# Routing ranks and counts in three wide products in place of nine narrow ones

## What is computed

```python
g_idx = jnp.argmax(g_logits, axis=-1)
e_sel = e_logits[rows, g_idx]
top_v, top_i = lax.top_k(e_sel, TOP_K_INNER)          # 2 of the 4 experts of the group
top_w = jax.nn.softmax(top_v, axis=-1) * g_w
e_idx = g_idx[:, None] * EXPERTS_PER_GROUP + top_i
combine = jnp.sum(jax.nn.one_hot(e_idx, N_EXPERTS) * top_w[..., None], axis=1)
for e in range(N_EXPERTS):                            # 16 experts
    h = jax.nn.silu(xt @ w_gate[e]) * (xt @ w_up[e])
    y = y + combine[:, e:e + 1] * (h @ w_down[e])
```

## Time and profile before

| | us |
|---|---|
| three executions | 620.52, 624.64, 624.0 |
| median | 624.0 |
| profiled execution | 623.38 |
| its span, first to last instruction | 620.3 |
| TensorE matmul busy in the span | 513.8 |
| VectorE busy | 250.8 |
| ScalarE busy | 149.7 |
| GpSimd busy | 66.9 |

### The profile page before, as it was taken

One profiled execution on the slowest core, in us unless ns is written; L12 is line 12 of the kernel. 1 busy time (PEld: TensorE's weight loads), 2 busy tenths in 40 slices (PEclk: granted clock), 3 DMA queues, 4 the chain that ended last, 5 costly groups with the idle time before them and its releaser, 6 DMA issues.

```text
span 620.3 us, 9275 instructions
## 1 busy us (share of the span) xinstructions
PE 513.8 (83%) x3600; PEld 394.0 (64%) x3601; DVE 250.8 (40%) x526; ACT 149.7 (24%) x283; POOL 66.9 (11%) x87
## 2 busy tenths in 40 slices
PE   4789978999989897999952999889997799787740
PEld 1789965988989897988652555546554455354410
DVE  2936956789464444414334111111120121111187
ACT  3435349775534422001010010000000010000010
POOL 4151730000000000000004300000000000000210
PEclk9999979999999997999955899999998899999795
DMA  8227891424257645495293299999999999999642
GB/s 227 98 73 216 230 309 42 136 70 137 69 166 279 234 166 173 155 402 215 92 412 109 96 392 365 396 408 406 393 386 403 399 403 422 409 424 423 230 106 85
DMA packets 55212, 157.47 MB, mean 254 GB/s; under 512 B 3558, under 2 KB 36034, under 8 KB 51076
## 3 DMA queue, kind: packets, MB, share of 16 engines
q1 hardware_dynamic: 46464, 135.11, 58.0%
q0 software_dynamic: 4896, 13.92, 7.7%
q10 hardware_dynamic: 3812, 7.88, 3.4%
HBM read 145.10 MB, written 11.78 MB: 253 GB/s over the span
## 4 chain that ended last, share of the span: by engine, by line
PE 60%; DMA 21%; DVE 7%; issue 4%; ACT 4%; SPq 2%; DVEq 1%; POOL 0%; POOLq 0%; ACTq 0%
PE bank L1043 21%; DMA expert_slots<-in_w_up 11%; PE bank L850 7%; PE bank L851 7%; PE bank L852 7%; PE bank L1004 7%; DMA expert_slots<-in_w_branch_rnn 3%; PE bank L1036 2%; SPq L606 2%; DMA expert_slots<-in_w_in 2%; DMA z_rows<-work 2%; PE bank L831 2%; PE bank L832 1%; PE bank L833 1%; DVE work L1445 1%
## 5 line engine op out<-in xcount | busy, mean ns | idle before, releaser
L1043 PE MATMUL bank<-expert_slots,work 128*64 128x256 f32 (+3 forms) x1584 | 191.9, 415 | 30.8 <-DMA expert_slots<-in_w_gate 9.4
L1043 PEld LDWEIGHTS bank<-expert_slots,work 128*64 128x64 f32 (+1 forms) x1584 | 110.8, 139 | 100.7 <-issue 46.3
L850 PE MATMUL bank<-z_high,weights_high 128*128 128x320 f32 (+1 forms) x320 | 101.6, 317 | 7.6 <-DVE weights_low L555 5.2
L852 PE MATMUL bank<-z_high,weights_low 128*128 128x320 f32 (+1 forms) x320 | 100.9, 315 | 0.0
L851 PE MATMUL bank<-z_low,weights_high 128*128 128x320 f32 (+1 forms) x256 | 79.5, 310 | 0.0
L555 DVE TENSOR_TENSOR weights_low<-expert_slots,weights_high 128x1024 fp32r<-128x1024 f32 (+1 forms) x54 | 61.1, 1157 | 38.1 <-ACT weights_high L549 37.9
L850 PEld LDWEIGHTS bank<-z_high,weights_high 128*128 128x128 f32 x320 | 61.8, 193 | 9.1 <-DVE weights_low L555 5.9
L1802 DVE SCALAR_TENSOR_TENSOR work<-work,bank 128x256 f32<-128x256 f32 (+1 forms) x18 | 7.3, 407 | 147.3 <-ACT work L1350 141.5
L549 ACT CAST weights_high<-expert_slots 128x1024 fp32r<-128x1024 f32 (+1 forms) x54 | 52.2, 987 | 48.2 <-PE bank L852 15.9
L852 PEld LDWEIGHTS bank<-z_high,weights_low 128*128 128x128 f32 x320 | 61.7, 193 | 0.0
L851 PEld LDWEIGHTS bank<-z_low,weights_high 128*128 128x128 f32 x256 | 48.0, 188 | 0.0
(11 more groups left out here) (264 smaller groups left out, 567.5 us busy)
## 6 DMA issues: line engine op xcount, KB each, us to landing
expert_slots<-in_w_gate SPq DMA_DIRECT2D x16, 2048.0 KB, 22.4
expert_slots<-in_w_up SPq DMA_DIRECT2D x16, 2048.0 KB, 28.1
expert_slots<-in_w_down SPq DMA_DIRECT2D x15, 2048.0 KB, 24.0
expert_slots<-in_w_in SPq DMA_DIRECT2D x19, 1024.0 KB, 5.3
expert_slots<-in_w_branch_rnn SPq DMA_DIRECT2D x4, 1024.0 KB, 6.4
expert_slots<-in_w_out SPq DMA_DIRECT2D x4, 1024.0 KB, 5.1
expert_rows<-work ACTq DMA_DIRECT2D x30, 128.0 KB, 8.4
expert_rows<-work POOLq DMA_DIRECT2D x6, 384.0 KB, 9.6
```

The source lines that it names most:

```text
L850: nc.tensor.matmul(o, wh[:, k, :], xh, start=(k == 0), stop=False)
L852: mm = nc.tensor.matmul(o, wl[:, k, :], xh, start=False, stop=(k == kk - 1))
L1043: mm = nc.tensor.matmul(bank[m * j:m * j + m, cols], lhsT(k), rhs(k, j), start=(k == 0), stop=(k == kk - 1))
```

## The change

The nine products become three. The first multiplies `before` with all three tiles of `e_sum` at once (48 columns). VectorE makes a new table `e_upto` with running sums of `e_sum` over the tiles: tile 0, tiles 0 and 1, all three. The second product adds `ones` times the first two running sums to the ranks of tiles 1 and 2 (32 columns), and the third makes the counts from the last running sum (16 columns). The second and third wait for the new table, which raises `chosen` a second time. The new table takes 48 more numbers per partition in the scratch area; what is laid out behind it there moves by as much.

```diff
         logit = rt.take(3, 20)
-        e_sum = rt.take(3, NE)
+        e_sum, e_upto = rt.take(3, NE), rt.take(3, NE)
...
             pe.wait_ge(chosen, 1)
             b = S.claim(pe, "ranks")
-            for j in range(3):
-                for i in range(j):
-                    nc.tensor.matmul(b[:, NE * j:NE * j + NE], ones, e_sum[:, i, :], start=(i == 0), stop=False)
-                nc.tensor.matmul(b[:, NE * j:NE * j + NE], before, e_sum[:, j, :], start=(j == 0), stop=True)
-            for i in range(3):
-                mm = nc.tensor.matmul(b[:, NE * 3:NE * 4], ones, e_sum[:, i, :], start=(i == 0), stop=(i == 2))
-            mm.then_inc(S.f_full("ranks"), 1)
+            chosen_flat = e_sum.rearrange("p j e -> p (j e)")
+            nc.tensor.matmul(b[:, 0:3 * NE], before, chosen_flat, start=True, stop=False)
+            pe.wait_ge(chosen, 2)
+            nc.tensor.matmul(b[:, NE:3 * NE], ones, e_upto[:, 0:2].rearrange("p j e -> p (j e)"), start=False, stop=True)
+            nc.tensor.matmul(b[:, 3 * NE:4 * NE], ones, e_upto[:, 2, :], start=True, stop=True).then_inc(S.f_full("ranks"), 1)
...
             tt(e_sum, e_sum, bc(cst("valid").unsqueeze(2), 3, NE), ALU.mult).then_inc(chosen, 1)
+            dve.wait_ge(chosen, 1)
+            step(V.tensor_copy(e_upto[:, 0], e_sum[:, 0]))
+            alone(tt(e_upto[:, 1], e_sum[:, 0], e_sum[:, 1], ALU.add))
+            tt(e_upto[:, 2], e_upto[:, 1], e_sum[:, 2], ALU.add).then_inc(chosen, 1)
```

## The result

The changed kernel took 621.54 us in the median of 12 executions (618.17 to 628.77), and the kernel before, run beside it, 626.08 us (620.52 to 631.0). The ratio is 0.9933 with a 95% interval of 0.9906 to 0.9959: 2.6 to 5.9 us less, which is within the 1% that was set as the bound. The forecast of 620.9 us is met to 0.6 us and the range of 618 to 624 holds the time. The gain, though, was forecast as 2.5 us and came out as about 4. Two misses stand behind the close hit: the three executions shown first lay low in the scatter of the kernel before, and the change gave more than the sum says. That the two nearly cancel is luck.

A forecast was written before the change was run, and what follows sets the result against it. The experts' weight stream bounds the kernel, its start set by a routing chain without slack, with nine products on the path. Three products start line 1734 2.52 us earlier: 623.38 - 2.52 = 620.86, forecast 620.9 us, range 618.0 to 624.0.

The forecast's parts named there:

- What bounds the kernel: Whole kernel: experts' weight stream decides; routing ahead has no slack from line 1734, where the nine products are the path.
- The price of a product: TensorE's ranks: 0.214 us per record, 0.43 us per product, set by weight columns, also with 48 moving columns.
- The rival by moving columns: Ranks' products: a record's price is proportional to its moving columns, gain only 1.28 us, time 622.1; chance 0.06.
- the sum of 2.52 us for the path: Routing: line 1734 starts at 322.77 us instead of 325.29, and the end moves by as much.
- VectorE's three instructions: Copy and two sums ahead of the second product: stall it 0.06 us; the weights' five, 0.49 later, stay covered.
- The load of expert 3: SP's issue that starts the weight stream: about 2.5 us earlier after the end of `e_sum`.
- the sooner rise: First expert's products: clock rises 2.8 us after their start instead of 5.1, 1.1 us gained, 619.7; chance 0.10.
- the 4.5 of the rival: First expert's products: clock rises later; wholly at the low level they take 4.5 us more, 625.4; chance 0.05.
- The stream: Experts' weights: bytes and order unchanged, so its 227 us stay as long and move as a whole.
- The rival that it hides the gain: Weight stream: a rate 1% slower costs 2.3 us, as much as the gain, time 623.2; chance 0.13.
- The base: Start of the sum: the profiled execution, 623.38 us, 0.62 under the median of 624.0.
- The time outside the span: Around the 620.3 us span of the profiled execution: 3.08 us, carried in the base without a change.

The follow-up runs named there:

- the last kernel: Changed kernel plus wide products (512 columns) in three routing gaps and 50 products of 32 weight columns at program start; median 620.73 us, ratio 0.9932.

## Why the prediction was right, and where its sizes were off

**What bounds the kernel.** Right. The three places that it named are where the time went: the nine products on the path, the routing without slack behind them, the stream that moves as a whole. Six products put back take the gain away, and nine more add 3.84 us to the path.

**The price of a product.** Right. It follows the weights and not the moving columns. The starts lie 0.50 and 0.44 us apart for 48 and 32 moving columns, and eighteen narrow products add 3.84 us over nine, 0.427 each; 0.43 was taken. The records of 32 weight columns in the kernel with 50 products at the start come 0.055 us apart, a quarter of that of 128. The rival by moving columns would have had the second product start no sooner than three times 0.43 us after the first. The record itself gets slightly longer, 0.67 us for the two of 48 columns against 0.59 for 16, but the next one starts in spite of it. Of the sum of 2.52 us for the path 2.49 were measured.

**VectorE's three instructions.** Right. They start 0.24, 0.33 and 0.53 us after line 1721, as worked out; the stall at the second product is 0.50 - 0.43 = 0.07 us against 0.06; VectorE's idle time falls to 0.44 against 0.42. The weights' five, 0.49 us later, stay covered: the kernel with the three instructions and nine products has the old path of 4.40 us.

**The load of expert 3.** Expected 2.5 us earlier after `e_sum`, and 3.46 earlier in the profile. The further 1.0 is the scatter of the clock: the products of the first expert took 8.48 us here, and 10.12 in another profile of the same kernel. With both levels known it can be worked out when the clock rose: wholly at the high level the 64 records take 7.13 us (the kernel with wide products), and each microsecond at the low level costs half of one, so a duration of 7.13 + r/2 has its rise r after the start. The kernel before's 9.65 gives 5.0; 8.48 gives 2.7, and the window above, 0.55 from 344 to 345, says the same; 10.12 gives 6.0. So the sooner rise happened in one execution, with 1.2 us, and a later one in another, but with 0.5 us and not the 4.5 of the rival. Both are part of the scatter of one program, and should have stood in the range and not in the chances.

**The stream.** Its rate and share stayed, 397 GB/s and 1.01. Its length up to the start of expert 14's down products lies between 219.4 and 220.1 us in the profiles of before and of the changed kernel, without an order by kernel. The rival that it hides the gain did not come about: the kernel with six products ahead, which has only the moved path, keeps 2.65 ± 0.65 us of it to the end.

**The base.** Mis-sized. The sum starts at 623.38 us, the profiled execution, and the text compares it with a median of 624.0 from three. Over 100 executions the mean is 626.07 ± 0.32. The four executions that I had are from the lower half of a scatter of 3.2 us, so that a range built on them lay too low; from the mean of the 100 the same sum gives 623.55, and the rival price by columns, 1.28 us of gain, would have given 624.8, outside the range.

**The time outside the span, and what is not on the path.** Here a step failed, and the hit hides it. The prediction took the 3.08 us around the span, and the pace of all instructions that are not edited, as the same before and after. They are not. The changed kernel gives 4.1 ± 0.5 us, its path 2.5. The kernel with the same path and the old length of TensorE's list gives 2.65 ± 0.65, and between it and the changed kernel lie 1.44 ± 0.71. In the 0.45 us outside the span this difference is plain, since that time scatters little and goes with the place of the loop: means of 2.5 to 2.75 us, with a standard deviation of 0.3 to 0.4, in the five kernels with as many products ahead of the loop as before, 2.1 in the changed kernel and the one with its loop 256 instructions on, 1.85 to 1.88 in the five at other places, both with at most 0.06. The remaining 1.0 ± 0.7 us in the span are not shown in a stage: the waits at an expert's first line differ by 2.3 to 3.6 us between the two places, but the stream's length doesn't. That it is the place as well is argued from this row and from the loop's far larger effects at other places.

The same oversight cost me expectations in the other direction, above all that of the kernel with wide products, whose 48 instructions cost 51 us. That the change came out on the good side of this is luck, of which nothing in the profile of before spoke.

The Trainium skill has a rule that bears on this ("Runtime: NRT & Kernel Launch", section "Instruction fetch mechanics"): instructions are refilled in blocks of 256, in sequence, and a taken branch whose target is outside the window held makes the engine wait for a fetch. The runs agree with it as far as they go: a shift by 256 brought the changed kernel's waits back, both lines with long stalls stand behind a branch, and the instruction queue moved 58 packets instead of 29 where they cost 51 us. That it is the fetch that TensorE waits for is not shown by a row. By the same section the crossing of a block is mostly hidden; for the branches of this loop the runs show that it depends on the place: 51 us lost at one, 21 us of stalls at another, 3.0 to 3.7 at a third.

## What to carry to other kernels

Where narrow fp32 products stand on a path, count products and not columns: three with 48, 32 and 16 moving columns cost a third of nine with 16, and running sums on an engine that waits anyway cost the path nothing: here 0.49 us of them went into 3.42 us of idle time. Where an engine's program has a loop, an edit ahead of it also moves the loop, so a gain or a loss of some microseconds, or of 50, can come from the number of instructions alone; compare with a kernel of the same length in which the new work lies off the path, and look at the instruction queue's packets. And before making a sum against one execution, ask how many executions its base rests on: here the median of three was 2 us low, and one pair of profiles had the wrong sign.

## What the runs showed of the hardware

- Twelve narrow products at the program's start, mostly in a gap, made the kernel 57 us slower than the changed one (678.67 ± 1.30 against 621.98 ± 0.43), by moving the loop 48 instructions. With the loop 40 instructions further the time is 627 to 631, with it 256 further than in the changed kernel 620.
- Narrow products, even in an unbroken row, did not raise TensorE's clock: 3.84 us busy out of 4 at a granted 0.50 in the ranks, and 7.86 out of 8 at 0.50 in the kernel with eighteen products (323 to 331 us). With products on 512 columns in the gaps the granted clock was 1.00 through the whole routing, which then took 24.78 us from `e_sum` to the load of expert 3 instead of 27.78 to 29.14; and it was gone again at 341.2 us in the last kernel, after a stretch in which TensorE was busy 0.10 us of one. In total this was worth 1.7 ± 0.9 us across chips, less than the profiles promise, and stays open as a gain.
- Of the six stalls at the turning in the kernel with eighteen products, 21.0 us in all, the first (2.42 us, right ahead of the load of expert 3) and the last (3.19 us of it, from 597.85 us, stand in the chain that ended last) are on the path; the total lies 5.4 ± 1.1 us above before, where the added products make 3.85.
- The time outside the span, which I took for a constant, differs by 0.75 us between programs (2.6 and 1.86) and goes with the place of TensorE's loop.
